# Eight weight buffers for the experts and a rearranged router stretch in a two-block transformer kernel

## The reference, cut to what matters

```python
merged = concatenate([rms_norm(attn, g_attn_out), rms_norm(lru, g_lru_out)], axis=-1)
x = x + gt1 * (merged @ w_out)
h = rms_norm(x, g_ffn) * (1.0 + sc2) + sh2
logits = h @ w_router + b_router
top_vals, top_idx = top_k(logits, 4); gates = softmax(top_vals)
# for each expert e, on the tokens that chose it:
gu = xb @ w_gu[e] + b_gu[e]
gate = minimum(gu[:, :1024], 7.0); up = clip(gu[:, 1024:], -7.0, 7.0)
y = ((up + 1.0) * gate * sigmoid(1.702 * gate)) @ w_down[e] + b_down[e]
x = x + gt2 * segment_sum(y * gate weight)
```

## Time and profile before

| | us |
|---|---|
| median of 3 runs | 2139.41 (2137.29 to 2143.17) |
| the profiled execution, its own time | 2145.34 |
| its span, first to last instruction | 2143.5 |
| PE busy | 2037.6 (95%) |
| DVE busy | 601.2 (28%) |
| ACT busy | 307.7 (14%) |
| POOL busy | 61.5 (3%) |
| DMA queue of SP, share of 16 engines | 68.1% |

### The profile page before, as it was taken

How to read it: one execution, slowest core, us unless ns; L and a number is a source line. 1 busy time by engine, 2 the same in 40 slices (tenths; PEclk the granted TensorE clock), 3 DMA queues, 4 the chain that set the end, 5 groups by cost and what they waited for, 6 DMA issues and landing times.

```text
span 2143.5 us, 24297 instructions
## 1 busy us (share of the span) xinstructions
PE 2037.6 (95%) x10031; PEld 1170.2 (55%) x10031; DVE 601.2 (28%) x1190; ACT 307.7 (14%) x697; POOL 61.5 (3%) x68
## 2 busy tenths in 40 slices
PE   8988999999998999999999999999999999999997
PEld 7766678856866768864854333333333333333332
DVE  0368453312167540002472111111111101111112
ACT  1324210000233410000340000000000000000001
POOL 0022000000012100000000000000000000000000
PEclk9979899999988999999998999999999999999999
DMA  7430068874422035435427999999999999999996
GB/s 304 157 119 1 1 235 307 342 262 178 148 89 79 1 138 197 174 145 193 172 92 293 396 428 429 428 429 429 428 429 428 429 428 429 429 428 429 428 429 295
DMA packets 44271, 598.72 MB, mean 279 GB/s; under 512 B 5056, under 2 KB 5360, under 8 KB 8464
## 3 DMA queue, kind: packets, MB, share of 16 engines
q1 hardware_dynamic: 44208, 597.82, 68.1%
HBM read 596.73 MB, written 1.07 MB: 279 GB/s over the span
## 4 chain that ended last, share of the span: by engine, by line
PE 76%; DMA 16%; DVE 6%; issue 1%; ACT 1%; SPq 0%; DVEq 0%; ACTq 0%
PE ps L1951 16%; DMA ring<-in_stream 16%; PE ps L1242 14%; PE ps L1263 7%; PE ps L1999 7%; PE ps L376 6%; PE ps L1925 3%; PE ps L1940 2%; PE ps L390 2%; PE ps L1169 2%; PE ps L2036 2%; PE ps L1476 1%; PE ps L777 1%; PE ps L1641 1%; PE ps L789 1%
## 5 line engine op out<-in xcount | busy, mean ns | idle before, releaser
L1951 PE MATMUL ps<-ring,HT 128*64 128x512 f32 x2176 | 483.2, 596 | 28.8 <-DMA ring<-in_stream 27.9
L1951 PEld LDWEIGHTS ps<-ring,HT 128*64 128x64 f32 x2176 | 152.2, 137 | 354.2 <-issue 285.5
L1242 PE MATMUL ps<-XT,ring 128*128 128x256 f32 (+1 forms) x1536 | 305.9, 362 | 3.3 <-DVE XT L313 3.3
L1242 PEld LDWEIGHTS ps<-XT,ring 128*128 128x128 f32 x1536 | 272.0, 190 | 36.6 <-DVE XT L313 3.7
L1999 PE MATMUL ps<-SB,HT 128*64 128x512 f32 x1088 | 247.7, 609 | 0.9 <-ACT HT L2061 0.9
L1999 PEld LDWEIGHTS ps<-SB,HT 128*64 128x64 f32 x1088 | 76.7, 139 | 169.0 <-issue 169.0
L2110 DVE TENSOR_SCALAR HT<-ps 128x512 f32<-128x512 f32 x34 | 23.5, 692 | 460.9 <-PE ps L1951 460.9
L1263 PE MATMUL ps<-ring,HT 128*128 128x512 f32 x352 | 151.7, 592 | 0.0
L2053 ACT ACTIVATE HT<-HT 128x512 f32<-128x512 f32 x34 | 21.4, 630 | 801.4 <-DVE HT L2110 801.4
L376 PE MATMUL ps<-XT,ring 128*128 128x256 f32 x576 | 126.4, 383 | 1.3 <-DMA ring<-in_stream 1.3
L2122 DVE TENSOR_TENSOR HT<-ps,TOK 128x512 f32<-128x512 f32 x34 | 23.5, 692 | 368.4 <-PE ps L1999 368.4
(11 more groups left out here) (419 smaller groups left out, 1795.5 us busy)
## 6 DMA issues: line engine op xcount, KB each, us to landing
ring<-in_stream SPq DMA_DIRECT2D x210, 2048.0 KB, 20.5
SB<-in_stream SPq DMA_DIRECT2D x68, 2048.0 KB, 19.8
SB<-in_ln SPq DMA_DIRECT2D x8, 512.0 KB, 9.5
CST<-in_const SPq DMA_DIRECT2D x1, 1362.0 KB, 5.4
PAR<-in_layer SPq DMA_DIRECT2D x2, 558.5 KB, 11.2
X<-in_x SPq DMA_DIRECT2D x1, 1024.0 KB, 5.0
HN<-in_head_norm SPq DMA_DIRECT2D x2, 512.0 KB, 12.0
SB<-mod_rows SPq DMA_DIRECT2D x2, 512.0 KB, 4.5
```

Of the source, the lines that this page charges most:

```text
L1242: m = pe.matmul(ps[:, 2 * (f % 2) + a, j * T + cols.start:j * T + cols.stop], w[:, k, a, j * P:(j + 1) * P], XT[:, k, cols], start=k == 0, ...
L1951: m = pe.matmul(ps[HD * half:HD * (half + 1), a, :], XE[:, 2 * b + k, q * SLOTS_E:(q + 1) * SLOTS_E], w[:, k, a, half, :], start=False, st ...
```

## The change

Eight things change, most of them between 1078 and 1150 us of the span.

1. The down slots of odd items get buffers of their own (`moe_buffer`): eight buffers, in `SB` at 0, 4096, 8192 and 12288. To make room `XT` moves into `SB`. `moe_second_sp` loads the two down slots of item 1 as soon as its expert is known, then its four gate/up slots. From item 2 on gate/up slots wait as before, down slots for the item two before.
2. The shift is no longer added to the rows by POOL (`modulated_pool` goes, and with it one load of modulation rows); it is added as the gathered rows leave PSUM. That copy moves from ACT to DVE (`moe_gather_dve`, `moe_gather_one_dve`).
3. The last attention unit and the last gate product stand ahead of all four attention pieces of the output product.
4. The sum of squares of the LRU half is first halved by an addition on DVE (`lru_square_dve`), so PE needs two products for a tile and not four.
5. The bias products of item 0 move ahead of the selection; one filler of 512 columns stays instead of three.
6. In `router_dve` the selection matrix of item 0 (`EP0`) is made ahead of the count of items; on PE the gather of item 0 is split, its first half ahead of that count's product, its second half behind the turn of the ranks.
7. The first owner row (`EOW`, L1811) is written in the mixer stretch.
8. The final gain and `b_down` are loaded later, into `PAR` and `HN`.

```diff
             sp.wait_ge(S("x_done"), 4 * DEPTH)
-            sp.dma_start(LNW, dram["gains"][2:3, :].broadcast_to([P, D])).then_inc(S("gain_loaded"), 16)
-            sp.dma_start(BD[0:NE, :], dram["b_down"]).then_inc(S("par2_loaded"), 16)
             moe_first_load(sp, 4)
             for b in range(2):
...
                 moe_first_load(sp, b)
+            sp.dma_start(LAST_GAIN, dram["gains"][2:3, :].broadcast_to([P, D])).then_inc(S("gain_loaded"), 16)
             sp.wait_ge(S("x_ready"), 2 * DEPTH + 1)
             moe_first_load(sp, 5)
+            sp.wait_ge(S("par2_loaded"), 48)
+            sp.wait_ge(S("h_tile"), 2)
+            sp.wait_ge(S("h_ready"), 2)
+            sp.dma_start(BD[0:NE, :], dram["b_down"]).then_inc(S("par2_loaded"), 16)
...
-        def modulated_pool(pool, t):
-            pool.wait_ge(S("mod_rows"), 80)
-            pool.wait_ge(S("h_tile" if t == 0 else "h_ready"), 2)
-            nc.gpsimd.tensor_tensor(HF[:, t, :], HF[:, t, :], MOD[3], ALU.add).then_inc(S("h_rows"), 1)
         def gated_pool(pool):
+            pool.wait_ge(S("mod_rows"), 64)
             pool.wait_ge(S("items"), 1)
-            pool.wait_ge(S("h_rows"), NT)
             nc.gpsimd.tensor_copy(MOD[5][HD:P, 0:512], MOD[5][HD:P, 512:1024]).then_inc(S("h_rows"), 1)
             pool.wait_ge(S("par2_loaded"), 64)
-            pool.wait_ge(S("h_rows"), NT + 1)
+            pool.wait_ge(S("h_rows"), 1)
             nc.gpsimd.tensor_tensor(BD[0:NE, :], BD[0:NE, :], MOD[5][0:NE, :], ALU.mult).then_inc(S("h_rows"), 1)
...
         def merge_sum_pe(pe, a):
-            pe.wait_ge(S("merge_sq"), 2 + a)
-            for t in range(NT):
-                for k in range(4):
+            pe.wait_ge(S("merge_sq"), 2 + 2 * a)
+            for t in range(NT):
+                last = (3, 1)[a]
+                for k in range(last + 1):
                     m = pe.matmul(ps[:, SS_BANK[a], t:t + 1], (ATT_SQ, RA)[a][:, k, t * P:(t + 1) * P], cst("ones")[:, 0:1],
-                                  start=k == 0, stop=k == 3)
+                                  start=k == 0, stop=k == last)
...
+        def lru_square_dve(v):
+            v.wait_ge(S("merge_sq"), 3)
+            nc.vector.tensor_tensor(RA[:, 0:2, :], RA[:, 0:2, :], RA[:, 2:4, :], ALU.add).then_inc(S("merge_sq"), 1)
...
             m.then_inc(S("counts"), 1)
-            clock_pe(pe, 3, 512)
+            pe.wait_ge(S("par2_loaded"), 48)
+            for a in range(2):
+                moe_bias_pe(pe, 0, a)
+            clock_pe(pe, 1, 512)
             pe.wait_ge(S("selected"), 1)
             strict, ones = cst("pairs")[:, 0:P], cst("ones")[:, 0:P]
...
+            pe.wait_ge(S("moe_p"), 1)
+            pe.wait_ge(S("h_tile"), 2)
+            pe.wait_ge(S("h_ready"), 2)
+            moe_gather_one_pe(pe, 0, range(4))
             pe.wait_ge(S("nxt"), 1)
             pe.matmul(ps[0:NE, 6, P:P + 1], cst("pairs")[0:NE, P:P + NE], NXT, start=True, stop=True).then_inc(S("item_end"), 1)
             for t in range(NT):
                 m = pe.transpose(ps[0:NE, 2, t * P:(t + 1) * P], RNK[:, t, :], ident)
-            m.then_inc(S("rank_t_ps"), 1)
-            pe.wait_ge(S("moe_p"), 1)
-            pe.wait_ge(S("h_rows"), NT)
-            moe_gather_one_pe(pe, 0)
+            m.then_inc(S("router_turn"), 1)
+            moe_gather_one_pe(pe, 0, range(4, KT)).then_inc(S("moe_xe_ps"), 1)
             pe.wait_ge(S("gates"), 1)
             for t in range(NT):
                 m = pe.transpose(ps[0:NE, 7, t * P:(t + 1) * P], GT2[:, t, :], ident)
-            m.then_inc(S("gates_t_ps"), 1)
+            m.then_inc(S("router_turn"), 1)
             pe.wait_ge(S("owner"), 1)
             pe.matmul(ps[0:1, 6, 256:256 + NITEM], cst("part")[0:NE, :], OH, start=True, stop=True)
             m = pe.matmul(ps[0:1, 6, 384:384 + NITEM], ones[0:NE, 0:1], OH, start=True, stop=True)
             m.then_inc(S("owner_ps"), 1)
             pe.wait_ge(S("moe_xe"), 1)
-            pe.wait_ge(S("par2_loaded"), 64)
-            for a in range(2):
-                moe_bias_pe(pe, 0, a)
             moe_gate_up_pe(pe, 0, 0, 0, (0,))
...
-            v.wait_ge(S("rank_t_ps"), 1)
+            v.wait_ge(S("router_turn"), 1)
             I(nc.vector.tensor_copy(RNKT[0:NE, :], ps[0:NE, 2, 0:T]))
+            moe_gather_one_dve(v, 0)
...
-        MOE_BUF = [slot(S_MOE + b) for b in range(RING)] + [view(SB, at, [SLOT]) for at in (6080, 10176)]
-        moe_arrived = [arrived[(S_MOE + b) % RING] for b in range(RING)] + [S("moe_down_low"), S("moe_down_high")]
+        MOE_BUF = [slot(S_MOE + b) for b in range(RING)] + [view(SB, at, [SLOT]) for at in (8192, 12288, 0, 4096)]
+        moe_arrived = [arrived[(S_MOE + b) % RING] for b in range(RING)] + [S("moe_down_even_low"), S("moe_down_even_high"),
+                                                                           S("moe_down_odd_low"), S("moe_down_odd_high")]
+        def moe_buffer(n, b):
+            return b + 2 * (n % 2) if b >= RING else b
         def moe_first_load(sp, b):
             sp.dma_start(MOE_BUF[b], dram["stream"][S_MOE + b]).then_inc(moe_arrived[b], 16)
-        def moe_load(sp, i, b, freed):
-            sp.wait_ge(S("moe_slot"), freed)
-            sp.dma_start(MOE_BUF[b], dram["stream"][bass.ds(i * ITEM_SLOTS + S_MOE + b, 1), :, :]
-                         .rearrange("a p n -> (a p) n")).then_inc(moe_arrived[b], 16)
+        def moe_load(sp, i, n, b):
+            to = moe_buffer(n, b)
+            sp.dma_start(MOE_BUF[to], dram["stream"][bass.ds(i * ITEM_SLOTS + S_MOE + b, 1), :, :]
+                         .rearrange("a p n -> (a p) n")).then_inc(moe_arrived[to], 16)
         def moe_expert(sp, i):
             return sp.value_load(ITI[0:1, bass.ds(i + 8, 1)], min_val=0, max_val=NE - 1)
         def moe_item_sp(sp, it, q):
-            e = moe_expert(sp, it * 2 + q + 1)
-            for b in range(ITEM_SLOTS):
-                moe_load(sp, e, b, it * PAIR_SLOTS + ITEM_SLOTS * q + b + 1)
+            e = moe_expert(sp, it * 2 + q)
+            for b in range(RING):
+                sp.wait_ge(S("moe_slot"), it * PAIR_SLOTS + ITEM_SLOTS * (q - 1) + b + 1)
+                moe_load(sp, e, q, b)
+            for b in range(RING, ITEM_SLOTS):
+                sp.wait_ge(S("moe_slot"), it * PAIR_SLOTS + ITEM_SLOTS * (q - 2) + b + 1)
+                moe_load(sp, e, q, b)
+        def moe_second_sp(sp):
+            e = moe_expert(sp, 1)
+            for b in range(RING, ITEM_SLOTS):
+                moe_load(sp, e, 1, b)
+            for b in range(RING):
+                sp.wait_ge(S("moe_slot"), b + 1)
+                moe_load(sp, e, 1, b)
         def moe_sp(sp):
             last = moe_last_pair(sp)
+            moe_second_sp(sp)
             with sp.Fori(0, last) as it:
-                for q in range(2):
+                for q in (2, 3):
                     moe_item_sp(sp, it, q)
-            moe_item_sp(sp, last, 0)
         def need_moe_slot(pe, it, q, b):
-            before = (S_MOE + b) // RING if b < RING else 0
-            pe.wait_ge(moe_arrived[b], it * 32 + 16 * (before + q + 1))
+            if b < RING:
+                pe.wait_ge(moe_arrived[b], it * 32 + 16 * ((S_MOE + b) // RING + q + 1))
+            else:
+                pe.wait_ge(moe_arrived[moe_buffer(q, b)], it * 16 + 16 * (q // 2 + 1))
...
+        def moe_gather_dve(v, n, half):
+            v.wait_ge(S("moe_xe_ps"), n)
+            nc.vector.tensor_tensor(XE[:, 4 * half:4 * half + 4, :], ps[:, 2, :].rearrange("p (k s) -> p k s", k=4),
+                                    SHIFT[:, 4 * half:4 * half + 4].unsqueeze(2).broadcast_to([P, 4, P]), ALU.add
+                                    ).then_inc(S("moe_xe"), 1)
+        def moe_gather_one_dve(v, q):
+            v.wait_ge(S("moe_xe_ps"), q + 1)
+            nc.vector.tensor_tensor(XE[:, :, q * SLOTS_E:(q + 1) * SLOTS_E], ps[:, 4 + q, :].rearrange("p (k s) -> p k s", k=KT),
+                                    SHIFT.unsqueeze(2).broadcast_to([P, KT, SLOTS_E]), ALU.add).then_inc(S("moe_xe"), 1)
...
+            moe_gather_one_dve(v, 1)
+            v.wait_ge(S("h_rows"), 1)
             with v.Fori(0, last) as it:
                 base = it * PAIR_SLOTS
                 moe_rows_dve(v, base + 6)
                 moe_pick_dve(v, it * 2 + 2)
                 moe_hidden_dve(v, base + 10, it * 2 + 2)
                 v.wait_ge(S("moe_pt_ps"), it * 2 + 2)
+                for half in range(2):
+                    moe_gather_dve(v, it * 2 + 3 + half, half)
                 moe_weigh_dve(v, it * 2 + 2)
...
-            pe.wait_ge(S("nsa_out"), DEPTH + 1)
-            pe.wait_ge(S("att_raw"), first + 4)
-            mix2_pe(pe, 0, 1, 0)
             attention_turn_pe(pe, first + 3)
             rg_pe(pe, range(3, 4))
             attention_out_pe(pe, first + 3)
-            mix2_pe(pe, 0, 1, 1)
+            pe.wait_ge(S("nsa_out"), DEPTH + 1)
+            pe.wait_ge(S("att_raw"), first + 4)
+            for c in range(2):
```

(7 more changed lines are left out.)

112 lines of the change are left out of this document (50 added, 62 removed).

## The result

The changed kernel takes 2130.0 us (median of 20 runs) where the kernel before takes 2138.7 (20 runs, side by side): a ratio of 0.9961, 95% interval 0.9951 to 0.9971. It is faster, by 8.7 us and not by 18.3. One of the 20 runs took 9834.64 us, for a reason that no trace shows; it carries no weight in a median. The profiled execution of the changed kernel has a span of 2133.5 us, 10.0 under that of the kernel before; its own time of 2136.2 lies 6.2 us above the median, that of the kernel before 5.9 above the one shown ahead. Up to 1098 us both profiles have the same time at half clock (95.4 us before, 95.5 now), so the two spans can be compared.

What follows compares the result with a forecast made beforehand. The experts' weight stream was taken as the bound, its gapless start set by PE's router path. A 15.4 us shift on PE plus 2.9 from buffers gave 18.3: 2139.4 - 18.3 = 2121.1 us, range 2114 to 2131.

Steps and rivals of the forecast that it cites:

- What bounds the kernel, and the stream: Experts' stage: ends when its weights have arrived, 4.89 us a slot; gapless from item 3's first slot after the change.
- 2.9 from the buffers: Experts' weight stream: item 2's down slots need not wait for PE, adding 2.9 us to the gain.
- 2.6 + 1.7: End of the mixer: LRU output earlier removes PE's wait, 2.6 us; the product behind it at full clock, 1.7 us.
- the sum of squares 0.67: End of the mixer: second sum of squares with 8 records in place of 16, forecast 0.7 us.
- POOL 1.05 and 1.4: Mixer end and selection: removing POOL's two additions unblocks DVE; first worth 1.05 us, 0.9 taken; second 1.4.
- I take the full clock: Without PE pauses the clock stays full: 1.7 us at the mixer piece, 2.9 for the gather, 1.6 for the slot.
- PE is free at 1120.2. It just fits.: Selection wait: bias and one filler take 2.80 us, so PE is free as the selection is ready at 1120.3.
- The gather's 2.9 and the slot's 1.6: Router to first slot: gather 2.9 us and first slot 1.6 us shorter at full clock; 0 each if it falls.
- the 15.4: PE's shift at the first slot's end: 7.3 selection + 3.6 bias + 2.9 gather + 1.6 slot, in us.
- the clock rival: Router stretch: clock falls all the same, losing 2.9 + 1.6 and 0.2; gain 13.6, 2125.8 us; chance 0.22.
- The other rivals: Shift not handed on: gain 2.9, 2136.5 us, chance 0.07. Stream slower: at 3% 2148.7 us, chance 0.04.
- bias 3.6: Just ahead of the first slot: item 0's bias is gone from there, gaining 3.6 us.

Runs made afterwards that it cites:

- six buffers: Changed kernel with the earlier kernel's six-buffer addressing and load order: 2134.4 us, ratio to the kernel before 0.9976.
- mixer order back: Changed kernel with last attention unit and gate product back behind one piece of the output product: 2133.8 us, ratio to the kernel before 0.9974.
- five fillers in the kernel before: Kernel before with five 512-column products in place of three in the wait for the selection, run twice: 2139.5 and 2135.7 us.
- bias and three F: Changed kernel with three 512-column filler products behind the bias in place of one: 2126.1 us, ratio to the kernel before 0.9934.
- three F and the bias moved back: Changed kernel with item 0's bias behind the gathers again and three 512-column fillers in the selection wait, run twice: 2124.9 and 2127.0 us.
- the version with the lowest medians: Changed kernel plus one 512-column filler between the two tokens' logits and one ahead of the bias, run twice: 2123.0 and 2122.3 us.
- F ahead of the bias alone: Changed kernel plus one 512-column filler ahead of the bias, none between the tokens' logits, run twice: 2131.5 us both times.

## Why the prediction was wrong

**What bounds the kernel, and the stream.** Right. 4.89 us a slot, 2.0 us to the first bytes, gapless from item 3's first slot, tail unchanged, 2.9 from the buffers: the rest is 997.3 in the kernel before and 997.1 with six buffers, 994.0 to 994.4 in most others with eight. Where it is 992.7 there is no low stretch between S and item 3's first slot; the others have one of 3.4 us, and where the rest is some 2 us longer (996.4 with the mixer order back, 999.1 with five fillers in the kernel before) it is one of 6.8.

**The end of the mixer, POOL.** Right in the profiled execution: 2.6 + 1.7 (a wait of 2.98 to one of 0.35, 5.37 to 3.70), the sum of squares 0.67, POOL 1.05 and 1.4. The selection is ready 7.17 us earlier, forecast 7.3. The 1.7 was partly luck: "without that pause I take the full clock" does not hold in five of 15 profiles.

**"PE is free at 1120.2. It just fits."** The step that failed, and with it "I take the full clock". They rested on one idea: that the clock falls after a pause, so that work put into the pause keeps it up. The clock fell at 1116.7, in the second token's logits, with no pause ahead (PE busy 10.86 of the 11 us before 1116). PE came 2.9 us late for the selection (1.75 for the bias, 1.07 for the filler). The gather's 2.9 and the slot's 1.6 did not come. About 1.0 more went on the small products and the 256-column filler. Together 8.4 of the 15.4. That the median of 2130.0 lies inside the range (2114 to 2131) is owed to the allowance for the clock rival at its upper end, not to the forecast.

**The rival.** "The clock falls in the router stretch all the same" is what happened, and its reason, thin work without an idle moment, fits the trace; no run shows that it is the cause. Its price, 4.7 us, was mis-sized: 8.4 was lost, since the fall came ahead of the bias and not behind the selection (the 2.9 us for the late PE stand in no term of that price). The Trainium skill, page "TensorE: Matmul & The Clock Gate", section "What's actually happening", has the clock set by how busy the engine has been; read as the share of busy time, this trace contradicts it (21.00 of 21 us busy, clock at half). The other rivals did not occur: the shift was handed on whole, and the rate stayed at 428 to 430 GB/s.

**The bias moved up.** The fall lies ahead of the bias, so the bias did not bring it; what stands behind the fall sets how long it lasts. With the same fall 4.0 to 4.3 us behind R, the stretch takes 26.57 us with bias and one F, 24.48 with bias and three F, 22.78 with three F and the bias moved back. So 2.1 us of the difference belong to the two dense products that the bias replaced, and 1.7 to its place. With dense products on either side of it and in the logits it fits at full clock (19.65), as reckoned. Of these 19.65 about 1.9 are the two added products; without them it would be 17.8, an estimate. The forecast's terms for this stretch (POOL's second 1.4, bias 3.6, gather 2.9, slot 1.6) make 27.4 - 9.5 = 17.9. So they were sized right for a clock that holds, and no profile held it with the changed kernel's own order.

**Open.** What decides between executions of one program whether the clock falls is not shown by any run; nor is how often the version with the lowest medians loses it. The sign ahead of the router leaves a rival untested: the profiles that won the mixer's 1.7 us are those whose clock falls in the second token's logits, so the terms of mixer and router may not simply add, and a single profile of a variant says little beside one of the other kind. That the fall follows thin runs is a reading that fits the profiles once they are seen; it did not foretell that the clock would fall again behind the bias with two fillers ahead of it. The pause matters as well (five fillers in the kernel before held the clock in one profile of two); the two were not parted cleanly. The order of the gather was not tried by itself.

## What to carry to other kernels

A product that only fills isn't free room: before another piece takes its place, price that piece and everything behind it at both clocks. Price a rival on the clock from the earliest place at which it can fall, not from the place in the old trace. And where the clock differs between executions, split profiles at fixed points of the program, take at least two, compare those whose clock was alike ahead of the stretch, and let the median of many runs decide.

## What the runs showed of the hardware

- The clock was at half for 20.5 us (changed kernel) and 23.9 (F ahead of the bias alone, second profile) while PE had no idle time; the work was mostly products of 32 to 128 columns and the bias on 32 rows, with one F, in the second case two, a filler of 256 columns and the start of the slot among it. In the logits the records are 16 in 1.87 us. Three F ended with the clock up in both profiles that had them behind a fall (4.17 us with the first part at half clock, 5.49 for those behind the bias).
- Two executions of one program differed by 10.5 us in 30 us of it (18.74 and 29.21).
- The clock fell behind a pause of 0.35 us in five profiles (5.39 or 5.40 us for the product behind it) and did not behind the same pause in ten (3.70).
- A GpSimd product of 128x1024 stretched a DVE addition from 0.69 to 1.75 us, also where the two touch different tiles.
